# The modulation's partition sum on TensorE: one fp32 product, or two fp32r halves against two columns of ones

## What is computed

```python
c_act = jax.nn.silu(c)
for l in range(DEPTH_2):
    mod = c_act @ ada_w[l] + ada_b[l]
    sh1, sc1, g1, sh2, sc2, g2, sh3, sc3, g3 = jnp.split(mod, N_ADA, axis=-1)
    h = modulate(x, norm_g[l, 0], sh1, sc1)
    x = x + 0.5 * g1[:, None] * swiglu(h, ff_w13[l, 0], ff_w2[l, 0])
    ...
```

## Time and profile before

| | before |
|---|---|
| device time, median of 3 | 1575.82 us |
| profiled execution, its own time | 1585.44 us |
| its span | 1583.7 us |
| PE busy | 1470.7 us (93%) |
| DVE busy | 1070.5 us (68%) |
| ACT busy | 727.0 us (46%) |
| granted TensorE clock, mean | 0.962 |
| L1134 (the partition sums), PE records | 288, 35.9 us |
| HBM read | 311.99 MB |

### The profile page before, as it was taken

How to read it: one execution, slowest core, us unless ns; L and a number is a source line. 1 busy time by engine, 2 the same in 40 slices (tenths; PEclk the granted TensorE clock), 3 DMA queues, 4 the chain that set the end, 5 groups by cost and what they waited for, 6 DMA issues and landing times.

```text
span 1583.7 us, 18472 instructions
## 1 busy us (share of the span) xinstructions
PE 1470.7 (93%) x7116; PEld 1216.0 (77%) x7116; DVE 1070.5 (68%) x1438; ACT 727.0 (46%) x1064; POOL 67.7 (4%) x109
## 2 busy tenths in 40 slices
PE   4988789899999999989889999899998989899998
PEld 3776667788887888878778888688887868688886
DVE  3687675667677766776657666777767778676445
ACT  5444454544436434454454333444334756353443
POOL 4000000000001000010000000000000000000000
PEclk9999899999999999999699999999999999899999
DMA  7753052577766777846148779678776630475651
GB/s 250 257 204 112 28 181 84 187 265 266 277 228 194 264 263 261 265 165 180 55 158 290 251 257 255 207 241 283 256 238 214 179 110 1 133 241 171 208 187 70
DMA packets 189116, 314.25 MB, mean 198 GB/s; under 512 B 6960, under 2 KB 100455, under 8 KB 189031
## 3 DMA queue, kind: packets, MB, share of 16 engines
q1 hardware_dynamic: 148528, 231.82, 45.5%
q10 hardware_dynamic: 38678, 76.69, 13.4%
q0 software_dynamic: 1824, 4.57, 0.9%
HBM read 311.99 MB, written 1.07 MB: 198 GB/s over the span
## 4 chain that ended last, share of the span: by engine, by line
PE 79%; DVE 9%; ACT 4%; issue 3%; POOL 2%; DMA 2%; ACTq 0%; DVEq 0%; POOLq 0%
PE ps L998 23%; PE ps L1000 23%; PE ps L999 22%; PE ps L1007 5%; PE ps L1297 2%; DVE wlo L958 2%; PE ps L1134 1%; PE ps L1252 1%; ACT whi L949 1%; DVE xn L1704 1%; DMA qT<-in_ada_w 1%; DVE tmp L1738 1%; DVE rmax L2029 1%; DMA raw<-in_nsa_w_out 1%; DVE sp L2026 1%
## 5 line engine op out<-in xcount | busy, mean ns | idle before, releaser
L958 DVE TENSOR_TENSOR wlo<-raw,whi 128x2048 fp32r<-128x2048 f32 (+1 forms) x221 | 501.6, 2271 | 179.9 <-ACT whi L949 179.2
L998 PE MATMUL ps<-whi,aT 128*128 128x512 f32 (+1 forms) x1216 | 493.5, 406 | 36.3 <-DVE aTl L1726 28.1
L1000 PE MATMUL ps<-wlo,aT 128*128 128x512 f32 (+1 forms) x1216 | 480.4, 395 | 0.0
L999 PE MATMUL ps<-whi,aTl 128*128 128x512 f32 (+1 forms) x1216 | 479.6, 394 | 0.0
L949 ACT ACTIVATE whi<-raw 128x2048 fp32r<-128x2048 f32 (+1 forms) x221 | 418.7, 1895 | 118.9 <-PE ps L1000 81.1
L998 PEld LDWEIGHTS ps<-whi,aT 128*128 128x128 f32 x1216 | 234.6, 193 | 85.0 <-issue 41.2
L1000 PEld LDWEIGHTS ps<-wlo,aT 128*128 128x128 f32 x1216 | 234.2, 193 | 49.7
L999 PEld LDWEIGHTS ps<-whi,aTl 128*128 128x128 f32 x1216 | 235.3, 193 | 43.7
L998 PE MATMUL ps<-whi,hT 128*128 128x512 f32 (+1 forms) x524 | 200.2, 385 | 2.2 <-ACT z L1537 1.4
L1000 PE MATMUL ps<-wlo,hT 128*128 128x512 f32 (+1 forms) x524 | 197.4, 379 | 0.0
L999 PE MATMUL ps<-whi,hTl 128*128 128x512 f32 (+1 forms) x524 | 197.0, 378 | 0.0
(11 more groups left out here) (230 smaller groups left out, 1296.4 us busy)
## 6 DMA issues: line engine op xcount, KB each, us to landing
raw<-in_ff_w SPq DMA_DIRECT2D x176, 512.0 KB, 4.8
raw<-in_ff_w SPq DMA_DIRECT2D x44, 1024.0 KB, 5.2
qT<-in_ada_w ACTq DMA_DIRECT2D x36, 1024.0 KB, 6.1
pT<-in_ada_w ACTq DMA_DIRECT2D x36, 1024.0 KB, 7.3
raw<-in_w_up SPq DMA_DIRECT2D x16, 1024.0 KB, 5.7
raw<-in_w_down SPq DMA_DIRECT2D x16, 1024.0 KB, 5.0
raw<-in_w_in SPq DMA_DIRECT2D x9, 1024.0 KB, 7.2
raw<-in_w_ckv SPq DMA_DIRECT2D x8, 1024.0 KB, 5.4
```

The lines of the kernel that those rows point to most:

```text
L958: dve.tensor_tensor(wlo[:, slot, 0:m], raw[:, slot, 0:m], whi[:, slot, 0:m].bitcast(F32), ALU.subtract).then_inc(w_lo, 1)
L998: pe.matmul(out_ap, hi, w, start=start, stop=False)
L999: pe.matmul(out_ap, lo, w, start=False, stop=False)
L1000: return pe.matmul(out_ap, hi, wl, start=False, stop=stop)
```

## The change

The last term still writes `asum`. At age 6 a new step `ada_split` stands: ACT copies `asum` to `ahi` as fp32r, DVE subtracts `ahi` from `asum` into `alo`. At age 7 and 8 each 128 columns take two fp32r matmuls, `ahi` and `alo`, against two columns of ones instead of one fp32 matmul against one column; DVE reads every second column of the result. The wait of the last term for the previous piece's matmuls moves from DVE to ACT's copy. POOL sets two columns of ones and copies them to fp32r, where it set 128 columns.

```diff
         if 2 <= m["age"] <= 5:
-            return [("ada_q", dict(m, q0=2 * (m["age"] - 2), prev=self.ada_t))]
+            return [("ada_q", dict(m, q0=2 * (m["age"] - 2)))]
+        if m["age"] == 6:
+            return [("ada_split", dict(m, prev=self.ada_t))]
...
             def ada_out(m):
                 t = m["t"]
-                pe.wait_ge(ada_sum, m["n"] + 1)
+                pe.wait_ge(ada_lo, m["n"] + 1)
                 wait_free(pe, T, lambda j: t)
                 for c in range(2):
                     k = 2 * m["half"] + c
-                    last = pe.matmul(tbank(t)[:, c:c + 1], asum[:, k * P:(k + 1) * P], ones[:, 0:1],
-                                     start=True, stop=True)
+                    pe.matmul(tbank(t)[:, 2 * c:2 * c + 2], ahi[:, k * P:(k + 1) * P], ones_r[:, :], start=True, stop=False)
+                    last = pe.matmul(tbank(t)[:, 2 * c:2 * c + 2], alo[:, k * P:(k + 1) * P], ones_r[:, :], start=False,
+                                     stop=True)
                 last.then_inc(t_ready, 1)
...
+            def ada_high(m):
+                act.wait_ge(ada_sum, m["n"] + 1)
+                if m["prev"] is not None:
+                    act.wait_ge(t_ready, m["prev"] + 1)
+                act.activation(ahi[:, :], asum, ACT.Copy).then_inc(ada_hi, 1)
...
-                        if q == KC - 1 and m["prev"] is not None:
-                            dve.wait_ge(t_ready, m["prev"] + 1)
...
+            def ada_low(m):
+                dve.wait_ge(ada_hi, m["n"] + 1)
+                dve.tensor_tensor(alo[:, :], asum, ahi[:, :].bitcast(F32), ALU.subtract).then_inc(ada_lo, 1)
...
-                dve.tensor_tensor(mod[:, m["layer"], c:c + 2], tbank(m["t"])[:, 0:2],
+                dve.tensor_tensor(mod[:, m["layer"], c:c + 2], tbank(m["t"])[:, 0:3:2],
...
-            const(pool.memset(ones[:, :], 1.0))
+            const(pool.memset(ones[:, :], 1.0), True)
+            const(pool.tensor_copy(ones_r[:, :], ones[:, :]))
```

More of the change, by code:

```diff
@@ L698, in build @@
         ident = sb("ident", [P])
-        ones = sb("ones", [P])
+        ones = sb("ones", [2])
+        ones_r = sb("ones_r", [2], F32R)
+        ahi, alo = sb("ada_hi", [ADA_W], F32R), sb("ada_lo", [ADA_W], F32R)
         causal = sb("causal", [S])
@@ L757, in build @@
         ada_loaded, ada_sum = [sem(f"ada_loaded{i}") for i in range(2)], sem("ada_sum")
-        ada_mid = sem("ada_terms")
+        ada_mid, ada_hi, ada_lo = sem("ada_terms"), sem("ada_sum_hi"), sem("ada_sum_lo")
         t_ready, t_act, t_dve = sem("t_ready"), sem("t_act"), sem("t_dve")
@@ L963, in build @@
                 for t in (qT[:, :, :], pT[:, :, :, :].rearrange("p a b c -> p (a b) c"))]
-        N_PRM_DMA, N_SMALL, N_CONST = 12, 15, 15
+        N_PRM_DMA, N_SMALL, N_CONST = 12, 15, 16
         block = ctx.enter_context(nc.Block())
@@ L1540, in linear @@
                                 ada_load(m)
+                            elif what == "ada_split":
+                                ada_high(m)
                             elif what == "tables":
@@ L1577, in body @@
                             ada_load(e)
+                        elif what == "ada_split":
+                            ada_high(e)
                         elif what == "stage":
@@ L1948, in linear @@
                                 ada_out(m)
+                            elif what == "ada_split":
+                                ada_low(m)
                             elif what == "tables":
@@ L1983, in body @@
                             ada_terms(e)
+                        elif what == "ada_split":
+                            ada_low(e)
                         elif what == "ada_out":
```

## The result

The changed kernel takes **1597.8 us** (median of 4 runs, 1595.5 to 1601.0) against 1576.0 us for the kernel before beside it; the ratio of the two, over runs in the same state, is **1.0106** (95% interval 1.0074 to 1.0137). A second comparison, on another chip, gave 1.009 (1.0061 to 1.0119). The forecast was 1584.4 us, a ratio of 1.0055: slower by less than 1%. The ratio on record is not the quotient of the two medians (that is 1.0138 here and 1.0094 in the second comparison), and the text goes by the ratio. The direction was right, the loss came out at nearly twice its size, some 14 to 17 us by the ratios instead of 8.6. The median of 1597.8 us lies 2.8 us above the range that was given; by the ratio, 1575.8 x 1.0106 = 1592.5 us, the kernel lies inside it.

The account below looks back on a forecast made before the run. PE sets the pace in the streams; at edges and projection ends it waits for ACT and DVE chains. Terms 0 + 6.0 + 1.0 + 1.4 + 0.2 = +8.6 us on 1575.8 gave 1584.4 us, range 1573 to 1595.

Parts of the forecast that it names:

- PE's part: In PE's sums, four fp32r loads an age replace four fp32 loads at 0.12 us each: no change, 0 us.
- The upper bound of +4 us: Bound on the cost of PE's sums, if accumulating a pair adds 0.015 us.
- the lower of -5 us: Bound on the cost of PE's sums, if each of 288 loads takes 0.02 us less.
- rival 2: PE's sums cost by number of passes, so PE saves half of 34.6 us, 17.3: 1567 us; chance 0.09.
- The sign that the prediction gave: In the stream, four new loads should take 0.48 us; clearly other than that would make the forecast wrong.
- Splits in the streams: 29 of 36 pieces split inside the MLPs, where DVE and ACT have room: nothing added, 0 us.
- Rival 3: Splits do reach PE's pace in the streams, 29 x 0.69 = 20 us more: 1604 us; chance 0.03.
- The three flush waits: Copy and subtraction in series before PE's sums: `w_ckv` +2.2, `w_cq` +1.6, `hy_in` fourth unit +2.2 us, +6.0 together.
- The step that failed: Work behind the three flushes is in series, so their waits count whole, +6.0 us; half if later steps had slack.
- Rival 1: Clock falls behind the `w_cq` flush, scores and products up to 7.6 us longer: +16.2, 1592 us; chance 0.16.
- `hy_in`'s start: Subtraction between DVE's terms and weight split makes PE's sum 1.4 us late; +1.0 us counted, bounds 0.7 and 1.4.
- the MLP ends: Ends of `ff01` and `ff10`, where DVE has no idle time: one subtraction each, 2 x 0.69 = +1.4 us.

Follow-up runs that it names:

- two-loads kernel: Kernel before with only the sum's format changed: each block summed twice in fp32r from one tile, no copy, subtraction or new wait; ratio 0.9985.
- one-load kernel: Kernel before with one fp32r matmul per 128 columns, low half left out, no copy or subtraction; 1573.3 us against 1584.5, ratio 0.9907.
- the kernel without PE's wait: Changed kernel with copies and subtractions kept but halves unused: fp32 sums, PE waiting only for the last term; 1593.5 us, ratio 1.0055 against the kernel before.
- 33 split: Changed kernel with the three pieces split and summed at one unit left whole in fp32; 1588.1 us against 1586.8 for the kernel before, ratio 1.0011.
- 3 split: Changed kernel splitting only the three flush pieces, the other 33 summed in fp32; 1601.5 us, ratio 1.0091 against the kernel before.

## Why the prediction was right, and where it was too small

- **PE's part, 0.** Right. The change's matmuls and loads are 288 each, and the two-loads kernel puts the format at 0.9985 (0.9961 to 1.0008). The upper bound of +4 us is out (the interval ends at +1.3), the lower of -5 us is not excluded by times; the spacing of PE's starts, 0.36 us an age in both, makes it nothing. The price itself was read too high: the 0.48 us of the earlier trace rows begin with the load that runs beside the matmul ahead, so the sums cost PE 72 x 0.36 = 26 us and not 34.6, and half of that, rival 2's gain, 13 and not 17.3. The sign that the prediction gave, four new loads in 0.48 us, reads 0.58 from the first load to the one behind the four, in the changed kernel as in the two-loads one, without costing PE anything. **Rival 2** (price by passes, 1567 us) fell. By the rule of four passes that the prediction cites from the Trainium skill an age had to go from eight passes to four; no run shows such a gain, and the one-load kernel gains what its missing loads cost.
- **Splits in the streams, 0.** Right: 33 of them cost 1.0011 (0.9988 to 1.0034). **Rival 3** (1604 us) fell; the trace's closest look, the 200 us of the MLP, has PE's busy time equal to 0.01 us.
- **The three flush waits.** The waits themselves were right: 1.93 and 1.93 us at `w_ckv` and `w_cq`, 2.24 at `hy_in`, 1.18 at its start, 7.3 in all against 2.2 + 1.6 + 2.2 + 1.4 = 7.4. The brackets tell idle time before the instruction; against the kernel before, the starts moved by 2.1 and, from 0.79 after the last matmul to 2.31, by 1.5 us, and at `hy_in` from 0.12 to 2.52, by 2.4. The chain at `hy_in` was not quite the one drawn: DVE's last term ended there behind ACT's copy from PSUM, and ACT's new copy waited 0.20 us for it. The `hy_in` one, in the changed kernel:

```profile
731.42 0.63 ACT L1516 ACTIVATE ada_hi<-prow 128x512 fp32r<-128x512 f32 x1 [0.20 <-DVE prow L1932]
732.08 0.69 DVE L1938 TENSOR_TENSOR ada_lo<-prow,ada_hi 128x512 fp32r<-128x512 f32 x1 [0.69 <-ACT ada_hi L1516]
732.83 0.27 PE L1138 MATMUL ps<-ones_r,ada_hi 128*128 128x2 f32 x1 [2.24 <-DVE ada_lo L1938]
```

- **The step that failed** is the sentence "What follows each ... is in series, so I count all of it: +6.0 us. If the later steps had slack it could be half." It allowed for less than the whole, not for more. It took the transposes and projections behind the wait at their old length; they ran partly at 1.2 GHz. From the marks the three flushes cost 3.1, 5.0 and 2.9 us in the first trace of the change, 11.0 of its 11.5, where 2.2 + 1.6 + 2.2 were counted. With PE kept busy in the waits the stretches are longer by 2.2, 1.5 and 2.5 us, which is the counted sum, and the kernel's ratio, 1.005, is the forecast's 1.0055: without the clock's fall the forecast would have been right in size too.
- **Rival 1** had the mechanism, at another place and on another condition. It looked for the fall in the scores and products behind `w_cq`, for up to 7.6 us, and counted nothing at `w_ckv`, where it had read a low clock already; behind the `hy_in` flush it allowed for 2 to 4 us. But at `w_ckv` that fall began, before, only with the scores; with the wait it comes in the sums and transposes ahead of them, which had run at full speed. And the point from which it was to decide, a wait of the full 1.6 us at `w_cq`, is not one: with 1.93 us of idle time ahead of the sums the clock fell in one trace of the changed kernel and not in the other, while it fell after 1.31 us behind `w_ckv` in the kernel without PE's wait. In the scores behind `w_cq` the clock did not fall: the 7.7 us behind 258.29 in the changed kernel ran at 1.00. Its total, +16.2 us, is nearer the result (14 to 17) than the forecast's, but that is luck, for its 7.6 us lay in a place that lost nothing. A chance of 0.16 for it was too low: the profile had shown the clock to fall behind one of the two flushes already.
- **`hy_in`'s start and the MLP ends.** From 637.01 to 706.52, the mark right behind the split at the start of `hy_in`, the changed kernel lost 0.2 us and the one with 33 split 0.5: of the +1.0 there is at most half, as far as single traces tell. For the MLP ends +1.4 was counted, and here the marks are sharp. From 1006.73 to 1020.96, around the end of `ff01`, all seven traces of kernels that split the MLPs' pieces take 0.6 us more than the kernel before, and the four others the same. From 1201.29 to 1207.27, ahead of the end of `ff10`, it is 0.3 us more and again nothing in the others. So the term was there, at 0.9 of its 1.4 us; what follows may win some of it back. From a mark at the first MLP's begin (309.44) to 637.01 the changed kernel and the one with 33 split both lose 0.7 us, the one with 3 split none, the kernel before in its second trace 0.35. All of this is within what a comparison can tell (33 split: 1.0011).
- **Time and ratio.** The forecast was set against a median of 1575.8 us of three runs. In 70 later runs of the same program on three other chips the medians are 1584.4 to 1586.8, so medians of different chips are not to be compared. Beside the changed kernel's first four runs the kernel before took 1576.0 us, as in the forecast, so a shift of that base does not explain the 13 us by which the median missed; how much of them is the scatter of four runs stays open. By the ratio the forecast missed by 0.5% in the first comparison and 0.35% in the second, 6 to 8 us.

What stays open: what of the total the clock took in the later attentions. Between the marks at 730.59 and 819.45 the traces take from 7.1 us less to as much as that of before, and between 1173.76 and 1357.76 from 0.2 us less to 11.4 us more, the kernel before itself 4.6 more in its second trace. A single trace can't assign that; only the timed ratios can.

## What to carry to other kernels

Before a split format is paid for, count its weight loads against the old one's. Here, where one or two moving columns left only the load to pay, a format that needs as many loads gave nothing, and each load fewer gave some 0.11 us. Work added to engines with room cost nothing measurable in the stream, and its whole length and more where a stage ends: let the pieces that come due at such an end keep the short path. When a wait is put into a gap that PE already spends half idle, price what stands behind it at half the clock too. In these traces the clock fell behind most such waits, but not behind each.

## What the runs showed of the hardware beyond that

The clock moves a whole phase. From the mark at 730.59 to that at 819.45 the kernel before, and the one with 33 pieces split, with the same 446 matmuls:

```profile
730.59:819.45 88.86, 78.68 (x446) 69.52 (x446) 52.95 (x88) 38.88 (x71) 3.84 (x6) 0.85 0.43 136
```

```profile
730.48:812.26 81.78, 70.44 (x446) 62.06 (x446) 53.10 (x87) 38.42 (x71) 3.84 (x6) 0.96 0.49 148
```

That is 7.1 us for the same matmuls, at 0.85 against 0.96 of the clock. The two kernels differ in how the modulation is summed, but that is not what this shows: the kernel before itself took 86.04 us there in its second trace, at 0.90. By the Trainium skill (TensorE: Matmul & The Clock Gate, HAM oscillation) a TensorE that idles between bursts of work drops to half its clock again and again; its example waits for a DMA ahead of each burst. The same page (What's actually happening) calls the number of matmuls that run at the low clock when a kernel starts variable from run to run. The traces agree with the fall: 8.2 us at 0.96 and 12.5 at 0.73 behind `w_ckv` with the same work and a wait of 2 us more. And they show variation from run to run inside a kernel too: 11.8 us against 9.5 behind `w_cq` in two traces of one program.

A two-column fp32r sum costs its load: at the high clock such matmuls start 0.11 us apart, in the changed kernel's slow stretch behind `w_cq` 0.21 us. From its timeline at the start of `hy_in`, and behind `w_cq`:

```profile
715.61 0.25 PE L1139 MATMUL ps<-ones_r,ada_lo 128*128 128x2 f32 x1
715.72 0.25 PE L1138 MATMUL ps<-ones_r,ada_hi 128*128 128x2 f32 x1
715.83 0.25 PE L1139 MATMUL ps<-ones_r,ada_lo 128*128 128x2 f32 x1
...
249.05 0.35 PE L1138 MATMUL ps<-ones_r,ada_hi 128*128 128x2 f32 x1
249.26 0.35 PE L1139 MATMUL ps<-ones_r,ada_lo 128*128 128x2 f32 x1
```
